# Small float32 products of a hybrid decoder kernel, split over four column groups of TensorE

## What is computed

```
for l in range(2):
    h = rmsnorm(x, norm_mix[l])
    q, fx, ix, g, u = split(h @ w_in)                    # 5 x 512 columns
    f = lb + (1 - lb) * sigmoid(fx)                      # 4 heads x 128
    o, S = hgrn2_scan(silu(q), log(f), 1 - f, ix, S0)    # S_t = diag(f_t) S_{t-1} + k_t v_t^T; o_t = S_t^T q_t
    o = o * rsqrt(mean(o * o)) * hg_norm * silu(g)
    yp, new_buf = multiscale_pool(u, buf, ...)           # trailing means of 2/4/8/16 rows, minus the token, then a 128x128 map
    x = x + concat(o, yp) @ w_o
    h = rmsnorm(x, norm_ffn[l])
    x = x + (swiglu(h) if l == 0 else moe(h, router))    # d_ff 2816; 8 experts of 1408, top 2
return rmsnorm(x, norm_final), states, pool buffers
```

## Time and profile before

| | |
|---|---|
| time, median of 3 runs | 851.5 us (850.46 to 852.2) |
| the profiled execution's own time | 850.92 us |
| its span, first to last instruction | 849.0 us |
| mean granted clock of TensorE | 0.996 of full speed |
| PE busy | 832.6 us (98%), 5471 matmuls |
| PEld busy | 726.6 us (86%), 5471 loads |
| DVE busy | 681.3 us (80%) |
| ACT busy | 574.1 us (68%) |
| POOL busy | 169.5 us (20%) |
| DMA | 222.01 MB, 262 GB/s on average |

### The profile page before, as it was taken

One profiled execution on the slowest core, in us unless ns is written; L12 is line 12 of the kernel. 1 busy time (PEld: TensorE's weight loads), 2 busy tenths in 40 slices (PEclk: granted clock), 3 DMA queues, 4 the chain that ended last, 5 costly groups with the idle time before them and its releaser, 6 DMA issues.

```text
span 849.0 us, 14351 instructions
## 1 busy us (share of the span) xinstructions
PE 832.6 (98%) x5471; PEld 726.6 (86%) x5471; DVE 681.3 (80%) x837; ACT 574.1 (68%) x715; POOL 169.5 (20%) x147
## 2 busy tenths in 40 slices
PE   6999999999999999999999999999999999999996
PEld 6999999999999999999988777777777777777776
DVE  5899678777665547996888889898998989898964
ACT  6857765544544348577966878787878787787842
POOL 4430276555411132303800000000000000000001
PEclk9999999999999999999999999999999999999998
DMA  8843267555678526424495999999999999899911
GB/s 301 313 159 108 78 236 253 186 185 173 245 276 274 194 100 209 139 100 176 161 310 177 384 381 421 322 408 338 395 376 355 391 344 414 320 422 323 395 66 52
DMA packets 52404, 222.01 MB, mean 262 GB/s; under 512 B 6208, under 2 KB 6336, under 8 KB 51694
## 3 DMA queue, kind: packets, MB, share of 16 engines
q1 hardware_dynamic: 50670, 209.61, 67.4%
q0 software_dynamic: 960, 9.50, 3.0%
q10 hardware_dynamic: 720, 2.18, 0.6%
HBM read 214.25 MB, written 7.47 MB: 261 GB/s over the span
## 4 chain that ended last, share of the span: by engine, by line
PE 93%; DVE 3%; ACT 2%; issue 1%; DMA 1%; DVEq 0%; ACTq 0%
PE bank L1812 43%; PE bank L1498 12%; PE bank L1499 12%; PE bank L1500 12%; PE bank L1656 2%; PE bank L1523 2%; PE bank L1868 2%; PE bank L1784 1%; PE bank L1821 1%; DVE sb_w_lo L997 1%; ACT sb_w_hi L570 1%; DMA sb_raw<-in_in_units_dram 1%; PE bank L1581 0%; PE bank L1749 0%; PE bank L1648 0%
## 5 line engine op out<-in xcount | busy, mean ns | idle before, releaser
L997 DVE TENSOR_TENSOR sb_w_lo<-sb_raw,sb_w_hi 128x1024 fp32r<-128x1024 f32 (+1 forms) x116 | 173.6, 1497 | 61.7 <-ACT sb_w_hi L570 60.5
L1498 PE MATMUL bank<-at_act_hi,sb_w_hi 128*128 128x264 f32 x672 | 194.1, 289 | 8.1 <-DVE sb_w_lo L997 8.1
L570 ACT ACTIVATE sb_w_hi<-sb_raw 128x1024 fp32r<-128x1024 f32 (+1 forms) x116 | 127.1, 1101 | 96.0 <-PE bank L1500 94.0
L1499 PE MATMUL bank<-at_act_lo,sb_w_hi 128*128 128x264 f32 x672 | 191.5, 285 | 0.0
L1500 PE MATMUL bank<-at_act_hi,sb_w_lo 128*128 128x264 f32 x672 | 191.3, 285 | 0.0
L1812 PE MATMUL bank<-sb_w_hi,at_packed 128*96 128x512 f32 (+1 forms) x768 | 189.7, 375 | 0.2 <-DVE at_packed L1264 0.2
L1044 DVE TENSOR_TENSOR sb_w_lo<-at_raw_e,sb_w_hi 128x1408 fp32r<-128x1408 f32 (+1 forms) x112 | 159.7, 1447 | 27.0 <-ACT sb_w_hi L638 26.4
L638 ACT ACTIVATE sb_w_hi<-at_raw_e 128x1408 fp32r<-128x1408 f32 (+1 forms) x112 | 139.0, 1242 | 38.2 <-PE bank L1812 38.2
L1044 DVE TENSOR_TENSOR sb_w_lo<-sb_raw,sb_w_hi 128x1408 fp32r<-128x1408 f32 (+1 forms) x104 | 149.8, 1479 | 14.3 <-ACT sb_w_hi L638 14.3
L1812 PEld LDWEIGHTS bank<-sb_w_hi,at_packed 128*96 128x96 f32 x768 | 122.4, 161 | 38.1 <-DVE at_packed L1264 0.6
L638 ACT ACTIVATE sb_w_hi<-sb_raw 128x1408 fp32r<-128x1408 f32 (+1 forms) x104 | 130.3, 1259 | 32.7 <-PE bank L1812 32.5
(11 more groups left out here) (275 smaller groups left out, 1255.7 us busy)
## 6 DMA issues: line engine op xcount, KB each, us to landing
sb_raw<-in_moe_w_up_dram SPq DMA_DIRECT2D x36, 704.0 KB, 7.2
at_raw_e<-in_moe_w_down_dram SPq DMA_DIRECT2D x49, 512.0 KB, 7.0
at_raw_e<-in_moe_w_gate_dram SPq DMA_DIRECT2D x35, 704.0 KB, 9.2
sb_raw<-in_up_units_dram SPq DMA_DIRECT2D x44, 512.0 KB, 3.3
sb_raw<-in_moe_w_gate_dram SPq DMA_DIRECT2D x29, 704.0 KB, 9.2
sb_raw<-in_in_units_dram SPq DMA_DIRECT2D x39, 512.0 KB, 3.8
sb_raw<-in_moe_w_down_dram SPq DMA_DIRECT2D x39, 512.0 KB, 5.2
at_raw_e<-in_moe_w_up_dram SPq DMA_DIRECT2D x28, 704.0 KB, 6.2
```

The source lines that it names most:

```text
L570: act.activation(w_hi[s][:, 0:kts, :], raw[s][:, 0:kts, :], ACT.Copy).then_inc(hi_done, 1)
L997: dve.tensor_tensor(w_lo[s][:, 0:kts, :], raw[s][:, 0:kts, :], w_hi[s][:, 0:kts, :].bitcast(f32), ALU.subtract).then_inc(lo_done, 1)
L1498: pe.matmul(out[:, 0:T], w_hi[s][:, k, :], hi[:, c, :], start=(c == 0), stop=False)
L1499: pe.matmul(out[:, 0:T], w_hi[s][:, k, :], lo[:, c, :], start=False, stop=False)
```

## The change

A helper `by_groups(out, left, right, **flags)` takes the place of `pe.matmul` in the small float32 products. It cuts the stationary operand `left` into pieces of up to 32 columns, and gives each as a matmul of its own with `tile_position=(0, m0)`: piece m0 lies in the array's columns m0 to m0+31 and writes partitions m0 to m0+31 of the same output. The moving operand `right` is the same for all pieces. It is used for the scores, the picks, the past sums, the attention, the final state, the router and the last norm. The operands of 128 stationary columns become 4 matmuls, those of 88 become 3 (32, 32 and 24). 144 calls of the first kind and 33 of the second become 675 matmuls, each of two passes. Waits, semaphores, banks and the place in the queue stay.

```diff
+            def by_groups(out, left, right, **flags):
+
+                for m0 in range(0, left.shape[-1], 32):
+                    m = slice(m0, min(m0 + 32, left.shape[-1]))
+                    mm = pe.matmul(out[m, :], left[:, m], right, tile_position=(0, m0), **flags)
+                return mm
+
...
                     for h in range(HEADS):
-                        mm = pe.matmul(bank[score_bank(i)][:, 128 * h:128 * (h + 1)], left(h), right(h), start=True, stop=True)
+                        mm = by_groups(bank[score_bank(i)][:, 128 * h:128 * (h + 1)], left(h), right(h), start=True, stop=True)
                     mm.then_inc(scored, 1)
...
                     for g in range(4):
-                        mm = pe.matmul(bank[7][:, DEC * g:DEC * (g + 1)], pool_past[:, 128 * g:128 * (g + 1)], pick[0:rows, g, :], start=True, stop=True)
+                        mm = by_groups(bank[7][:, DEC * g:DEC * (g + 1)], pool_past[:, 128 * g:128 * (g + 1)], pick[0:rows, g, :], start=True, stop=True)
                     mm.then_inc(past_summed, 1)
...
-                            mm = pe.matmul(bank[2][:, c:c + 4], read_rows[:, g, 128 * h:128 * (h + 1)], ident[:, row:row + 100:33], start=True, stop=True)
+                            mm = by_groups(bank[2][:, c:c + 4], read_rows[:, g, 128 * h:128 * (h + 1)], ident[:, row:row + 100:33], start=True, stop=True)
...
-                    mm = pe.matmul(bank[6][:, hs], values[:, 0, hs], scores[:, 0, h, :], start=True, stop=True)
+                    mm = by_groups(bank[6][:, hs], values[:, 0, hs], scores[:, 0, h, :], start=True, stop=True)
...
-                    pe.matmul(bank[7][:, hs], values[:, 0, hs], scores_x[:, h, :], start=True, stop=False)
-                    mm = pe.matmul(bank[7][:, hs], values[:, 1, hs], scores[:, 1, h, ::-1], start=False, stop=True)
+                    by_groups(bank[7][:, hs], values[:, 0, hs], scores_x[:, h, :], start=True, stop=False)
+                    mm = by_groups(bank[7][:, hs], values[:, 1, hs], scores[:, 1, h, ::-1], start=False, stop=True)
...
                     for i, (t0, rows) in enumerate(TOKEN_TILES):
-                        mm = pe.matmul(bank[7][0:rows, N_EXPERTS * i:N_EXPERTS * (i + 1)], scaled_m[:, kt, t0:t0 + rows], router[:, kt, :],
+                        mm = by_groups(bank[7][0:rows, N_EXPERTS * i:N_EXPERTS * (i + 1)], scaled_m[:, kt, t0:t0 + rows], router[:, kt, :],
                                        start=(kt == 0 and i == 0), stop=(kt == KT - 1), skip_group_check=True)
...
-                            pe.matmul(bank[6][:, hs], kdecT[:, 0, hs], values[:, 0, hs], start=True, stop=False)
-                            mm = pe.matmul(bank[6][:, hs], kdecT[:, 1, hs], values[:, 1, hs], start=False, stop=True)
+                            by_groups(bank[6][:, hs], kdecT[:, 0, hs], values[:, 0, hs], start=True, stop=False)
+                            mm = by_groups(bank[6][:, hs], kdecT[:, 1, hs], values[:, 1, hs], start=False, stop=True)
...
                 for i, (t0, rows) in enumerate(TOKEN_TILES):
-                    mm = pe.matmul(bank[0][0:rows, i:i + 1], square_f[:, kt, t0:t0 + rows], ones[:, 0:1], start=(kt == 0 and i == 0), stop=(kt == KT - 1),
+                    mm = by_groups(bank[0][0:rows, i:i + 1], square_f[:, kt, t0:t0 + rows], ones[:, 0:1], start=(kt == 0 and i == 0), stop=(kt == KT - 1),
                                    skip_group_check=True)
```

## The result

The changed kernel takes a median of **852.1 us** against 851.26 for the kernel before, each over 22 executions; the ratio is **1.0013, interval [1.0008, 1.0019]**: 0.8 to 1.1 us slower, depending on whether medians or the ratio are taken. One execution of the changed kernel took 1175.9 us at a granted clock of 0.66; it and the few like it in later runs are left out of the ratios. The profiled execution took 851.45 (span 849.4), the one before 850.92 (span 849.0). The time lies within the range that I gave and within the 0.2% that I had called no change, but with this many executions the interval excludes both no change and the gain of 0.3 of my sum.

The account below looks back on a forecast made before the run. PE was taken to bound the kernel (98% busy, 93% of the last chain). Terms +8.3, -1.0 and -6.6 gave +0.7, less 1.0 net for hidden parts, -0.3 us; forecast 851.1, range 849.2 to 857 (forecast's own case: to 853.5).

Parts of the forecast that it names:

- the gain of 0.3 of my sum: Whole kernel: all costs and gains, less what waits hide, net -0.3 us.
- Term 1: Changing the array's shape around each stretch in groups: 0.33 us a stretch, 25 new stretches, +8.3 us.
- Term 2: Products streaming 128 float32 columns: 0.108 us a pass in groups against 0.112, 240 passes, -1.0 us.
- Term 3: Products streaming 1 to 8 columns (past sums, picks, router, last norm): 0.031 us a pass in groups, together -6.6 us.
- handing over: Rival, products in groups: a busy group holds up those behind it, starts 30 ns apart; slower, 856.1 us, chance 0.22.
- program order: Rival, products in groups: matmuls start strictly in queue order, a level takes 2.0; slower, 879 us, chance 0.07.
- cheaper switch: Rival, array shape changes behind short products: 0.13 us a switch in place of 0.33; faster, 846.1 us, chance 0.13.
- two signs of being wrong: Prices in the changed profile: short passes costing more than 0.06 us, or stretches paying other than 0.33.
- what is hidden: Waits at attention, `sided` and last norm absorb costs, a router gain is lost: net -1.0 us.
- The late scores: Rival, score levels: half of 17 pass 0.3 us on through DVE, +2.5; slower, 853.6 us, chance 0.08.
- The last norm: Kernel's end: only six of 18 passes count, -0.3 us; waits of 0.91 and 0.64 hide both shape changes, -0.3.

Follow-up runs that it names:

- picks1: Only the picks of layer 1 in groups, against the kernel before; 850.93 us in a single execution, kernel before 851.38 on that chip.
- picks0: Only the picks of layer 0 in groups, against the kernel before; 851.04 us in a single execution, kernel before 851.38 on that chip.
- hold_after: Changed kernel, with POOL's decay of the states in layer 1 waiting until DVE has made the last `mix_lo`; 851.75 us, ratio 1.0008 [0.9999, 1.0016].
- again: The changed kernel run once more without further edit, beside the kernel before; 852.12 against 851.28 us, ratio 1.0011 [1.0002, 1.002].

## Why the prediction was wrong

**What held.** *Term 1*, 0.33 a stretch: 0.31 measured, net of the 0.02 that the level's eight passes win at 0.109 for 0.112, so 0.33. That it is a property of the switch and not of DVE's wait is shown by the level alone, which waits for nothing. *Term 2*, 0.108 a pass of 128 columns in groups: the starts in the level's trace lie 7, 7, 6 and 89 ns apart (114 once, behind the first four), 109 a pass, against 112 at full width, so next to nothing to win, as I had it.

*Term 3*, 0.031 for a short pass: the picks' loads give (0.63 - 0.11 - 0.02) / 15 = 0.033 (one load and the stagger off), the router's (0.65 - 0.11 - 0.01) / 17 = 0.031. My number had been a choice between 0.028 and 0.112, and it lay at the right end.

The estimate that I had drawn from the Trainium skill, TensorEngine Tiling (Array Packing), section Instruction Overhead (60 cycles, 25 ns a matmul, 0.100 for four), doesn't hold for groups: the picks' 64 matmuls were over within 0.72 us, a start every 9 ns. Neither handing over (groups 30 ns apart, a level of 1.3) nor program order (2.0) came, so those rivals are out. The Trainium skill, TensorE: Matmul & The Clock Gate, part 3, says that matmuls keep program order in start and end; with the two passes of a call in a row, as I had read it, that doesn't agree with the level's 1.08 us. In what order the passes are issued, the trace doesn't tell. The cheaper switch is out with term 1.

The router, 5 x 0.33 - 2.4 + 0.2 = -0.55 by my sum, shows +1.05 to +0.23: -0.82. Neither of my two signs of being wrong came (short passes above 0.06, stretches other than 0.33): the prices were right, and what failed lies in the part on what is hidden.

**What failed** is one step: "*In layer 1 two score levels wait 0.23 and 0.30 for `sided`; DVE makes it without PE's last products, so PE coming later shortens these: -0.5.*" My terms give layer 1 about 10 x 0.33 - 0.5 - 1.9 - 0.1 - 0.5 = +0.3; the trace gives -0.03 at 118.2 to +1.05 at 410.3, **+1.08**. The wait of 0.23 went, as I had it. But level 7 didn't wait 0.30 less, it waited 0.71 longer: from 376.9 to 381.3 I had 0.31 - 0.30 = 0.0, and it is +0.79. I had followed the wait back by one instruction (`sided` needs no product of the last levels) and not by the engine: DVE's `sided` stands behind its `sb_w_lo`, that behind ACT's `sb_w_hi`, and that waits for PE to empty a buffer. PE's delay went round this ring and came back as 0.36.

The second half of the same error is in term 3: the picks' -1.3 a layer was counted as kept, though in both layers a wait for DVE follows a few units on. Picks1 and picks0 show the whole of it lost, 0.94 of 0.95 and 0.97 of 0.94. Then comes the joint behind POOL (see hold_after) that I had at nothing, +0.35 of the +0.42 between 381.3 and 401.4. (The layer's other terms together came out 0.36 under mine.) This joint depends on how long one DMA takes, so it differs between executions, and the median lies further above the kernel before (0.84) than the profiled execution does (0.53).

The changed kernel has six above 853.5, up to 854.26, where the kernel before has none above 852.31. For four of the six, with spans of 851.7 to 852.2, this joint is the likely cause, but only argued from one such trace (again, 853.25, span 851.3). The other two, 853.55 and 853.88, have spans of 850.5: 1.2 to 1.5 us of theirs lie outside the span, which this joint can't make. Their cause is open.

**The late scores** were a rival of mine at 0.08, with 853.6. That PE's lateness comes back through DVE is what came, though I had rejected it on account of the copies (`take`). In the timelines of DVE from 365 to 382 no copy waits for PE; it goes through the weights' ring, and at a smaller price.

**Layer 0** came out at -0.03 to -0.03, where my terms say +0.25. That the two are near each other is luck: from 48 to 76 DVE sets the pace, so that neither the levels' +1.5 nor the picks' -0.9 counted. What counts is where DVE's full stretch begins, and the past sums with their level moved that by -0.35; the final state then cost 0.29.

**The last norm** I had at -0.27. Through the experts PE stays at +0.18, and it starts to spread the result at 842.47 against 842.33, +0.14: the norm gives -0.04. The timeline of the changed kernel:

```profile
840.39 1.95 DVE L1424 TENSOR_SCALAR at_scaled_f<-sb_xT,sb_vecs 128x264 f32<-128x264 f32 x7
...
841.20 0.26 ACT L959 ACTIVATE sb_root<-bank,sb_eps 88x3 f32<-88x3 f32 x1 [0.58 <-PE bank L1477]
842.25 0.16 DVE L1463 RECIPROCAL sb_rstd_tok<-sb_root 88x3 f32<-88x3 f32 x1
842.47 1.35 PEld L1934 LDWEIGHTS bank<-sb_consts,sb_rstd_tok 88*128 88x128 f32 x6 [1.41 <-DVE sb_rstd_tok L1463]
```

ACT has the sums 0.6 sooner (841.20 against 841.81), but the reciprocal stands on DVE behind the products of L1424, which don't depend on them, so PE's wait grows from 0.64 to 1.41. It is a fourth joint of the same kind.

Behind it comes the largest part of the difference in span, and it isn't shown to be the change's. PE's spreading products, which no edit touches, before and changed:

```profile
842.33 1.26 PE L1927 MATMUL bank<-sb_consts,sb_rstd_tok 88*128 88x88 f32 x6 [0.55 <-DVE sb_rstd_tok L1463]
```

```profile
842.47 1.58 PE L1934 MATMUL bank<-sb_consts,sb_rstd_tok 88*128 88x88 f32 x6 [1.32 <-DVE sb_rstd_tok L1463]
```

The granted clock falls from 1.00 to 0.50 at 842.7 in the kernel before, in the middle of them, and at 842.0 in the changed kernel, ahead of them: 0.32 longer. Kernels that are alike in this part differ as much: in again and hold_after, with the last norm of the changed kernel, they took 1.58 (fall at 843.5, ahead of them) and 0.90 (844.6, behind them), in picks0 and picks1, with that of the kernel before, 1.58 and 0.90 too.

Adding up what PE's ends show, in the order layer 0, layer 1, router, last norm: 0.0, +1.08, -0.82 and -0.04, against my +0.25, +0.3, -0.55 and -0.27. With -0.03 at the start, -0.05 from the router to the experts and the clock's +0.32 that is +0.46, and the spans differ by 0.47. Layer 1 is what came out above my sum, by 0.8; the clock's 0.3 is read from the two profiled executions, and with the traces so far it is luck. One slip of mine changes nothing: the middle of 850.6 and 851.2 is 850.9, not 851.1.

## What to carry to other kernels

A share of 98% busy doesn't say that PE's work counts in full: take the waits that PE has left, however short, and ask of each whether the engine it waits for is itself free; where that engine is saturated (4.00 of 4.00 us) a gain of PE ahead of the wait is worth nothing and any work added to that engine counts in full, and where it is fed by PE through a ring of buffers, PE's delays can come back. Follow a wait back along the engine's queue, not only along the data. For 32-column groups on a kernel of full-width matmuls: a stretch costs 0.31 us to enter and leave, a short product with 128 stationary columns wins 0.08 us a pass and one with 88 wins 0.05, a product that streams 128 float32 columns wins next to nothing (0.003 a pass), so use them only where more than four short passes stand together (more than six with 88 columns), and not ahead of a joint. Before a difference of some tenths in span is explained, look at where the granted clock falls at the end of each trace.

## What the hardware showed that I had not expected

- Two elementwise operations of DVE, 0.78 us long, took 1.28 to 2.65 us while POOL was at work, and ended 0.64 us after POOL's block in each case; with POOL held back they took 0.78 again. The same 0.64 stands in all ten traces in which the block lasted 0.3 us or more into the pair. It goes both ways: POOL's block took 5.07 us in the traces where DVE was idle for most of it, and 6.12 in hold_after, where DVE was at work.
- A DMA that writes 16 KB to DRAM (`v_saved`) made POOL wait 2.8 to 4.9 us in the fourteen traces. The four longest (3.82, 4.08, 4.41, 4.88) are those of the kernels in which the attention's products are in groups and the levels are not late. Why is open; I haven't tried it.
- Matmuls in four groups went out every 9 ns when they stream 4 columns, and four by four, 109 ns from pass to pass, when they stream 128. In the run of 64 short ones no gap between two starts is above 32 ns.
- The granted clock fell from 1.00 to 0.50 at the end of each of the fourteen traces, between 839.4 and 846.0 us after the start. The same six matmuls took 0.90 us ahead of the fall (picks1, hold_after and two more) and 1.58 behind it.
